# Token halves in the transition to the mLSTM, and column sums issued inside the second halves

## The chip, the core and the metric

The kernel runs on one core of a Trainium2 chip. Its engines are TensorE (PE in the profile; PEld is its weight load), VectorE (DVE), ScalarE (ACT), GpSimd (POOL) and SyncE (SP), whose queue starts the loads from HBM. Each engine runs its own instructions in the order in which they are written, and semaphores tie them together. The metric is the device time of one launch in microseconds, lower is better.

## The reference

`reference` runs one block of a first network and then one block of a second on 512 tokens of width 1024, all in float32. The first puts 16 meta tokens ahead of them, so it works on 528 tokens until its mixer is done.

```python
h = concat(meta_tokens, x)                                                     # 528 tokens
h = h + 0.5 * rmsnorm(swiglu(rmsnorm(h, gn[0]), ffn_w_in[0], ffn_w_out[0]), gn[1])  # feed-forward 0
u = rmsnorm(h, gn[2])
h = h + rmsnorm(mlstm_mixer(u, ...), gn[3])                                    # z = u @ w_in; conv; scan; y @ w_out
h = h + 0.5 * rmsnorm(swiglu(rmsnorm(h, gn[4]), ffn_w_in[1], ffn_w_out[1]), gn[5])  # feed-forward 1
x = h[16:]
h = x + 0.5 * swiglu_2(rms_norm(x, ffn1_norm), ...)                            # feed-forward 2
h = h + concat(mla, retention) @ w_o
h = h + 0.5 * swiglu_2(rms_norm(h, ffn2_norm), ...)                            # feed-forward 3
return rms_norm(h, final_norm)
```

## The kernel before

Activations lie transposed: width on the 128 partitions in `KD` = 8 tiles, tokens along the free axis, 528 of them (`TOK`) in feed-forward 0 and the mLSTM, 512 (`SEQ`) after. A tile k of a buffer is `buf[:, k*TOK : (k+1)*TOK]`. Each float32 product is made of three matmuls on rounded high and low parts (`whi`, `wlo` of the weights; `xhi`, `xlo` of the activations). Weights come in units of 128 x 1024 into four slots (`raw`); ACT makes `whi` (`split_to`, line 584), POOL makes `wlo` (`pool_lo`, line 457), and PE frees a slot when it is through with a unit (`unit_done`).

Between two stages lies a transition. The last products of a stage, tiles m = 0 to 7, are squared by ACT (`sq`, line 790), scaled and kept by DVE (line 1613), and the squares are added up in `acc` (line 1609). PE turns `acc` and the last `sq` into column sums, with `ones` as one moving column (matmuls of 128x1 in PSUM bank 7); ACT takes the root, DVE the reciprocal, and PE spreads it over the partitions by transposes of `rcol`. This gives r of the output norm. Then DVE multiplies a value tile by r (`wa`), the residual `hT` is updated (k = 0 on DVE, k = 1 to 7 on POOL), ACT makes `xhi` and the square of `hT` (`sqbuf`), DVE makes `xlo`, and PE multiplies the first units of the next stage by `xhi` and `xlo`. The squares in `sqbuf` give the next norm in the same way (sums, root, reciprocal, spread, `rbc`). It is applied behind the product, so the first products of the next stage need only `xhi` and `xlo`, while what DVE does with them needs `rbc`.

There are three transitions that the change touches. The **first** goes from feed-forward 0 to the mLSTM (`act_norm`, `dve_res`, `pool_res`, `sum_out`, `first_tiles`): whole tiles of 528 tokens, no product before r is in `rbc`; six adds of `sum_square` on DVE leave two squares to sum, 10 matmuls, behind projection 2. The **second** (mLSTM to feed-forward 1) and the **third** (feed-forward 1 to feed-forward 2) work by halves of 256 tokens. `out_steps` splits the last 3 output tiles (second) or the last one (third; table `SPLIT`), so that the first half of all tiles is complete while PE still makes the second; `act_transition`, `dve_transition`, `pool_transition` and `first_halves` hold the order, which is written out by hand. In `first_halves` PE first multiplies three units by the first halves of k = 0 to 7 (72 matmuls; the third unit lags by 3 k), with the sums and the spread of the second half's r in between, and then by the second halves (9 matmuls for each k, 72 in all). `sum_squares` gives the column sums of the next norm in two parts: 12 matmuls that wait for `norm_summed`, which DVE raises with the last of its three pair adds (`pair_squares`) behind all of `xlo`, and 8 matmuls on the last two squares. Before, part 0 stands behind k = 6 and part 1 behind k = 7; the spread stands in the fourth unit (`halved`).

What follows the first transition is the short convolution: DVE takes projection m from PSUM (line 1714, needs `rbc` and `unit_done`) and runs four more instructions on it, for m = 0 to 7; projection m >= 3 waits for `z_ready` of m - 3, and the value products wait for `z_ready` 6, 7 and 8. What follows the others is `dve_ffn`: `scaled` (line 1398), `conv_gate(0)` (line 1377, needs unit 0), `conv_up(0)` (line 1386, needs a SiLU of ACT, line 631), and on, until the loop of fast products (line 2508) starts.

## Time and profile before

| | |
|---|---|
| time, median of 3 runs | 2060.98 us (2059.63 to 2065.14) |
| the profiled execution's own time | 2064.66 us |
| its span | 2062.9 us |
| PE busy | 1983.3 us (96%) |
| DVE, ACT, POOL busy | 1190.0, 949.8, 915.8 us |
| granted PE clock, mean | 0.982 of full |

The span is what the profile covers; 1.8 us lie around it. The chain of waits is the chain that ended last, followed back from the end. A matmul that is recorded as float32 with 128x1 counts twice in the records (20 records for 10 matmuls). The first transition lies at 401 to 439 us, the second at 653 to 702 us, the third at 1028 to 1076 us. The clock column PEclk is 1.0 at 2.4 GHz and 0.5 at 1.2 GHz.

### The profile page before, as it was taken

What the parts mean: (1) busy time and instruction counts of PE and PEld (TensorE: products, weight loads), DVE (VectorE), ACT (ScalarE), POOL (GpSimd) and SP (SyncE); (2) the same over time, 40 slices, a digit from 0 to 9 for tenths busy, and PEclk for the clock granted to TensorE, in tenths of its full rate; (3) what the DMA queues carried; (4) which work ended last, traced back from release to release, by engine and by line L of the source; (5) the groups of instructions that cost most, each with busy time, mean ns of one, the idle gap of its engine ahead of it and who ended that gap; (6) DMA issues with size and microseconds to landing.
All of it is one profiled execution on the core that took longest, in us unless ns stands there. A gap on an engine that the chain in (4) does not pass through costs nothing.

```text
span 2062.9 us, 36078 instructions
## 1 busy us (share of the span) xinstructions
PE 1983.3 (96%) x13216; PEld 1774.7 (86%) x13216; DVE 1190.0 (58%) x1674; ACT 949.8 (46%) x1623; POOL 915.8 (44%) x528
## 2 busy tenths in 40 slices
PE   7899999899999989999999999999999999999998
PEld 7899999887778889987888999787776678999787
DVE  5766650186255777781068778314856637777611
ACT  4466642233423456662245666324426444666522
POOL 4244454444314445555453556454442033555542
PEclk9999999989999999999999999999999999999999
DMA  5133333213212133333322333334321022333331
GB/s 158 52 102 102 102 108 88 82 45 92 72 42 82 52 92 102 108 99 105 97 63 71 105 109 112 93 102 98 91 57 31 22 71 67 108 110 103 103 101 53
DMA packets 342479, 177.89 MB, mean 86 GB/s; under 512 B 18651, under 2 KB 338006, under 8 KB 342382
## 3 DMA queue, kind: packets, MB, share of 16 engines
q1 hardware_dynamic: 340528, 175.46, 29.5%
q8 instruction: 68, 1.11, 0.2%
q10 hardware_dynamic: 1854, 1.07, 0.2%
q14 instruction: 29, 0.24, 0.0%
HBM read 174.42 MB, written 2.10 MB: 86 GB/s over the span
## 4 chain that ended last, share of the span: by engine, by line
PE 82%; DVE 6%; issue 5%; ACT 3%; POOL 2%; DMA 0%; SPq 0%; ACTq 0%; POOLq 0%; DVEq 0%
PE ps L2268 40%; PE ps L2508 33%; POOL wlo L457 2%; PE ps L2333 1%; DVE E L1722 1%; DVE xop_f L1398 1%; PE ps L3000 1%; PE ps L2982 1%; PE ps L2959 1%; PE ps L2296 1%; DVE xop L1424 1%; PE ps L2363 1%; DMA raw<-in_ffn_w_in 0%; DVE wa L1697 0%; PE ps L2963 0%
## 5 line engine op out<-in xcount | busy, mean ns | idle before, releaser
L457 POOL TENSOR_TENSOR wlo<-raw,whi 128x1024 fp32r<-128x1024 f32 x192 | 484.8, 2535 | 662.3 <-ACT whi L584 661.8
L2508 PE MATMUL ps<-xop,whi 128*128 128x256 f32 (+1 forms) x4032 | 725.9, 283 | 16.4 <-issue 7.8
L2508 PEld LDWEIGHTS ps<-xop,whi 128*128 128x128 f32 x4032 | 623.8, 190 | 18.5 <-issue 9.5
L2508 PE MATMUL ps<-xop,wlo 128*128 128x256 f32 (+1 forms) x2016 | 569.1, 282 | 0.0
L2508 PEld LDWEIGHTS ps<-xop,wlo 128*128 128x128 f32 x2016 | 382.4, 190 | 0.0
L520 POOL TENSOR_TENSOR wlo<-raw,whi 128x512 fp32r<-128x512 f32 x212 | 283.8, 1343 | 215.1 <-ACT whi L661 215.1
L2268 PE MATMUL ps<-xop,whi 128*128 128x512 f32 (+2 forms) x1148 | 329.9, 348 | 13.4 <-POOL wlo L457 8.3
L584 ACT ACTIVATE whi<-raw 128x1024 fp32r<-128x1024 f32 x176 | 183.5, 1052 | 260.6 <-PE ps L2268 252.4
L2268 PE MATMUL ps<-xop,wlo 128*128 128x512 f32 (+2 forms) x902 | 284.7, 347 | 0.0
L2268 PE MATMUL ps<-xhi,whi 128*128 128x512 f32 (+2 forms) x672 | 225.4, 369 | 17.1 <-DVE xlo L1333 5.5
L2268 PEld LDWEIGHTS ps<-xop,whi 128*128 128x128 f32 x1148 | 197.1, 189 | 45.9 <-POOL wlo L457 5.3
L661 ACT ACTIVATE whi<-stage 128x512 fp32r<-128x512 f32 x216 | 136.6, 632 | 196.4 <-DVE stage L1448 118.2
L2268 PE MATMUL ps<-xlo,whi 128*128 128x512 f32 (+2 forms) x672 | 218.0, 358 | 0.0
L2268 PE MATMUL ps<-xhi,wlo 128*128 128x512 f32 (+2 forms) x672 | 217.6, 357 | 0.0
L2268 PE MATMUL ps<-hid_r,whi 128*128 128x512 f32 (+2 forms) x656 | 207.0, 347 | 0.0
L520 POOL TENSOR_TENSOR wlo<-stage,whi 128x512 fp32r<-128x512 f32 x72 | 93.4, 1297 | 198.6 <-ACT whi L661 198.6
L2268 PEld LDWEIGHTS ps<-xop,wlo 128*128 128x128 f32 x902 | 158.4, 189 | 22.6
L2268 PEld LDWEIGHTS ps<-xhi,whi 128*128 128x128 f32 (+1 forms) x672 | 121.1, 194 | 42.5 <-issue 18.9
L2268 PEld LDWEIGHTS ps<-xlo,whi 128*128 128x128 f32 (+1 forms) x672 | 121.1, 193 | 19.2 <-issue 2.2
L2268 PEld LDWEIGHTS ps<-xhi,wlo 128*128 128x128 f32 (+1 forms) x672 | 120.6, 193 | 18.1
L661 ACT ACTIVATE whi<-raw 128x512 fp32r<-128x512 f32 x216 | 133.6, 618 | 0.1
L2268 PEld LDWEIGHTS ps<-hid_r,whi 128*128 128x128 f32 x656 | 115.4, 189 | 16.6
(377 smaller groups left out, 2744.2 us busy)
## 6 DMA issues: line engine op xcount, KB each, us to landing
raw<-in_ffn_w_in SPq DMA_DIRECT2D x88, 512.0 KB, 3.7
raw<-in_ffn_w_gate SPq DMA_DIRECT2D x44, 512.0 KB, 3.7
raw<-in_ffn_w_up SPq DMA_DIRECT2D x44, 512.0 KB, 3.7
raw<-in_ffn_w_out SPq DMA_DIRECT2D x32, 512.0 KB, 3.9
raw<-in_ffn_w_down SPq DMA_DIRECT2D x32, 512.0 KB, 3.8
raw<-in_a_w_in SPq DMA_DIRECT2D x24, 512.0 KB, 3.7
raw<-in_w_in SPq DMA_DIRECT2D x19, 512.0 KB, 3.8
raw<-in_ffn_w_out SPq DMA_DIRECT2D x16, 384.0 KB, 3.3
```

Source lines behind the costliest of these rows:

```text
L457: pool.tensor_tensor(wlo[:, u % SLOTS, :], raw[:, u % SLOTS, :], whi[:, u % SLOTS, :].bitcast(F32), ALU.subtract).then_inc(lo_done, 1)
L520: pool.tensor_tensor(operand(wlo, i, name), source, operand(whi, i, name).bitcast(F32), ALU.subtract) \
L584: act.activation(whi[:, s, :], raw[:, s, :], ACT.Copy).then_inc(hi_done, 1)
L661: ins = act.activation(operand(whi, i, name), source, ACT.Copy)
L1398: ins = v.scalar_tensor_tensor(out=x_halves(k, n), scalar=gain(name, g0 + k), in0=hT[:, k * TOK + o:(k + 1) * TOK].rearrange("p (a n) -> p ...
L1424: v.tensor_tensor(x_operand(xop, name, 1, n), x_operand(xop_f, name, 1, n), x_operand(xop, name, 0, n).bitcast(F32), ALU.subtract).then_in ...
L1722: link(v, "dve", v.scalar_tensor_tensor(out=cacc(b), in0=zpad(b)[:, j:j + TOK], scalar=w[j], in1=cacc(b), op0=ALU.mult, op1=ALU.add))
L2268: ins = pe.matmul(o, lhs[l], x[r], start=first and n == 0, stop=last and n == 2)
L2296: ins = pe.matmul(ps[:, 7, c:c + 1], buf[:, o0 + o:o0 + o + P], ones[:, 0:1], start=q == 0, stop=q == len(sources) - 1, skip_group_check=True)
L2333: ins = pe.matmul(ps[:, b, HW * half:HW * (half + 1)], w[l], x[r], start=half == 0 and k == 0 and q == 0, stop=k == KD - 1 and q == 2, ski ...
L2363: ins = pe.matmul(ps[:, 7, c + 1:c + 2], sqbuf[:, k * TOK + META + c * P:k * TOK + META + (c + 1) * P], ones[:, 0:1], start=k == 0 and c = ...
L2508: ins = pe.matmul(ps[:, bank_, 0:h], w[l][:, k * P:(k + 1) * P], x[r][:, k * h:(k + 1) * h], start=start and k == 0 and q == 0, stop=k == ...
```

## The change

The first transition gets the halves of the other two: `SPLIT` has an entry for it, its first half holds 272 tokens (meta tokens and 256), its second 256. `first_tiles` and `sum_out` go from that place, and the first three mLSTM units run in `first_halves`; its matmuls there stay at 264 columns. The `sum_square` adds go, so the next norm's sums are 15 and 10 matmuls instead of 10. In all three transitions `sum_squares` part 0 moves behind k = 1, part 1 behind k = 2 and the spread behind k = 3 of the second halves. In the second, DVE makes the steps of the split output tiles ahead of the first `xlo`, with the `acc` adds early; ACT makes `xhi` of k = 0 between the two weight splits.

```diff
-SPLIT = {1: 3, 2: 1}
+SPLIT = {0: 1, 1: 3, 2: 1}
...
+    def half_span(n, half):
+        return ((0 if n == TOK else META, META + HW), (META + HW, TOK))[half]
+    def half_chunks(n, half):
+        first = [(0, 0)] if n == TOK and half == 0 else []
+        return first + [(c + 1, META + c * P) for c in (2 * half, 2 * half + 1)]
...
-        pool_lo(pool, u, U_M1 + AHEAD)
-        pool_res(pool, 0, TOK)
-        pool_transition(pool, 1, U_M1 + AHEAD, FFNS[1]["u0"])
+        pool_transition(pool, 0, u, U_M1)
+        pool_transition(pool, 1, U_M1 + SLOTS, FFNS[1]["u0"])
...
     def act_transition(...)
         for q in range(2):
             if q < SPLIT[i] - 1:
-                act_out_step(act, i, SEQ, False, u0, per, None, KD + q)
+                act_out_step(act, i, n, False, u0, per, None, KD + q)
             split_to(act, u_next + 1 + q - AHEAD)
-        x_hi(0, 0)
-        x_hi(1, 0)
+            x_hi(q, 0)
...
     def dve_transition(...)
-                if half == 0 and SPLIT[i] == 3 and k in (2, 4):
-                    step(KD + k // 2 - 1)
+                if half == 0 and k == 2:
+                    for p in range(KD, first):
+                        dve_out_acc(v, i, n, p)
+                        out_value(p)
+                    dve_out_acc(v, i, n, first)
                 if half == 0 and k == 5:
-                    step(first)
+                    out_value(first)
...
     def first_halves(...)
         for k in range(KD):
             for b, u in zip(banks, units):
                 ins = multiply(b, u, k, 1)
                 if k == KD - 1:
                     ins.then_inc(unit_done, 1)
-            if k >= KD - 2:
-                sum_squares(pe, norm, k - KD + 2)
+            if k in (1, 2):
+                sum_squares(pe, norm, k - 1, n)
+            if k == 3:
+                spread(pe, {R0: N1, R1: N2, R2: N3}[rms])
...
     def pe_mlstm(pe):
-        first_tiles(pe, 1, TOK, (0, 2), (u0, u0 + 1))
-        for m in range(2, 8):
+        first_halves(pe, 0, R0, 1, (0, 2, 4), (u0, u0 + 1, u0 + 2))
+        for m in range(3, 8):
             pe.wait_ge(lo_done, u0 + m + 1)
-            if m == 3:
-                spread(pe, N1)
-            if m >= 3:
-                pe.wait_ge(s["z_ready"], m - 2)
+            pe.wait_ge(s["z_ready"], m - 2)
             project(pe, 2 * (m % 3), TOK, u0 + m, None).then_inc(unit_done, 1)
-            if m == 2:
-                sum_norm(pe, 1, TOK)
...
     def pe_ffn(...)
-        whole = NU_DOWN - (len(FFN_PIECES) if i == 1 else 0)
+        whole = NU_DOWN - (len(FFN_PIECES) if i in (0, 1) else 0)
...
     def prog_tensor(pe):
         pe_ffn(pe, 0, 0, N0)
-        sum_out(pe, 0, TOK)
-        spread(pe, R0)
-        pe.wait_ge(r_s["ready"], r_at[R0]["ready"] + 2)
         pe_mlstm(pe)
```

How the change moves instructions is shown at three places. The first is PE at the end of the third transition's `first_halves`, before (`sqbuf` holds the squares of the residual, `rcol` the reciprocals):

```order
L2333 MATMUL ps<-xhi,wlo 128x256
L2363 MATMUL ps<-ones,sqbuf 128x1 [waits norm_summed]
L2363 MATMUL ps<-ones,sqbuf 128x1 x11
L2333 MATMUL ps<-xhi,whi 128x256 [waits norm_x_ready]
...
L2363 MATMUL ps<-ones,sqbuf 128x1 [waits norm_sq_ready]
L2363 MATMUL ps<-ones,sqbuf 128x1 x7
L2268 MATMUL ps<-xhi,whi 128x512 [waits ffn_banks_free,lo_done]
```

Here the 12 matmuls that wait for `norm_summed` have 63 of the 72 second-half matmuls ahead of them and 9 behind. The same instructions after the change:

```order
L2332 MATMUL ps<-xhi,wlo 128x256
L2364 MATMUL ps<-ones,sqbuf 128x1 [waits norm_summed]
L2364 MATMUL ps<-ones,sqbuf 128x1 x11
L2332 MATMUL ps<-xhi,whi 128x256 [waits norm_x_ready]
...
L2364 MATMUL ps<-ones,sqbuf 128x1 [waits norm_sq_ready]
L2364 MATMUL ps<-ones,sqbuf 128x1 x7
L2332 MATMUL ps<-xhi,whi 128x256 [waits norm_x_ready]
...
L2391 MATMUL ps<-ident,rcol 128x128 [waits rms_recip]
L2391 MATMUL ps<-ident,rcol 128x128 x3
L2332 MATMUL ps<-xhi,whi 128x256 [waits norm_x_ready]
```

Now 18 of the 72 stand ahead of the wait and 54 behind it; 9 lie between the two parts of the sums, 9 between them and the spread, and 36 behind the spread.

The second place is PE where feed-forward 0 ends. Before, the mLSTM's first product (`xhi`, 128x264) comes behind all sums and the whole spread, and also waits for `rbc` (`rms_ready`):

```order
L2268 MATMUL ps<-hid_r,whi 128x264 x2
L2268 MATMUL ps<-xop,wlo 128x264 x2
L2296 MATMUL ps<-ones,acc 128x1 [waits out_sq_ready,out_acc_done]
...
L2388 MATMUL ps<-ident,rcol 128x16 [waits rms_recip]
L2390 MATMUL ps<-ident,rcol 128x128 x4
L2268 MATMUL ps<-xhi,whi 128x264 [waits lo_done,norm_x_ready,rms_ready]
```

After the change the sums of the first half stand among the products (`xop`, `hid_r`) of the last tile's second half:

```order
L2260 MATMUL ps<-xop,wlo 128x256
L2305 MATMUL ps<-ones,acc 128x1 [waits out_sq_ready,out_acc_done]
L2305 MATMUL ps<-ones,acc 128x1 x2
L2305 MATMUL ps<-ones,sq 128x1 x3
L2260 MATMUL ps<-xop,whi 128x256
...
L2316 MATMUL ps<-ident,rcol 128x16 [waits rms_recip]
L2316 MATMUL ps<-ident,rcol 128x128 x2
L2260 MATMUL ps<-xop,whi 128x256
```

Six column sums and three transposes have gone into the last output tile; four and two more stand in `first_halves`.

The third place is DVE in the second transition, first halves (`y` is the kept output, `wa` the tile scaled by r). Before:

```order
L1613 TENSOR_SCALAR y<-ps,vec 128x256 [waits out_sq_ready]
L1652 SCALAR_TENSOR_TENSOR xlo<-hT,vec,xhi 128x256 [waits norm_hi_ready]
L1647 TENSOR_TENSOR wa<-y,ps 128x256 [waits res_h_ready]
L1652 SCALAR_TENSOR_TENSOR xlo<-hT,vec,xhi 128x256 [waits norm_hi_ready]
L1647 TENSOR_TENSOR wa<-y,ps 128x256 [waits res_h_ready]
L1609 TENSOR_TENSOR acc<-acc,sq 128x256 [waits out_acc_done,out_sq_ready]
L1613 TENSOR_SCALAR y<-ps,vec 128x256 [waits out_sq_ready]
L1652 SCALAR_TENSOR_TENSOR xlo<-hT,vec,xhi 128x256 [waits norm_hi_ready]
L1647 TENSOR_TENSOR wa<-y,ps 128x256 [waits res_h_ready]
L1609 TENSOR_TENSOR acc<-acc,sq 128x256 [waits out_acc_done,out_sq_ready]
```

After:

```order
L1623 TENSOR_SCALAR y<-ps,vec 128x256 [waits out_sq_ready]
L1614 TENSOR_TENSOR acc<-acc,sq 128x256 [waits out_acc_done,out_sq_ready]
L1623 TENSOR_SCALAR y<-ps,vec 128x256 [waits out_sq_ready]
L1614 TENSOR_TENSOR acc<-acc,sq 128x256 [waits out_acc_done,out_sq_ready]
L1664 SCALAR_TENSOR_TENSOR xlo<-hT,vec,xhi 128x256 [waits norm_hi_ready]
L1659 TENSOR_TENSOR wa<-y,ps 128x256 [waits res_h_ready]
```

Both `acc` adds stand ahead of the first `xlo`, where the second stood behind the third.

## Rows read from the trace of the kernel before

**Rows 1.** The page: busy time of each engine, and the chain's shares.
```profile
PE 1983.3 (96%) x13216; PEld 1774.7 (86%) x13216; DVE 1190.0 (58%) x1674; ACT 949.8 (46%) x1623; POOL 915.8 (44%) x528
...
PE 82%; DVE 6%; issue 5%; ACT 3%; POOL 2%; DMA 0%; SPq 0%; ACTq 0%; POOLq 0%; DVEq 0%
```

**Rows 2.** Chain of waits, 400 to 445 us: start, length, what.
```profile
...
402.21 2.38 PE ps L2296 x20
...
434.04 2.14 PE ps L2296 x20
```

**Rows 3.** Timeline of PE: start, length, form, count, idle before, releaser.
```profile
400.96 0.40 PE L2268 MATMUL ps<-xop,wlo 128*128 128x264 f32 x2
...
411.21 0.78 PE L2268 MATMUL ps<-xhi,whi 128*128 128x264 f32 x2 [5.25 <-issue]
...
479.15 0.50 PE L2268 MATMUL ps<-whi,xhi 128*128 128x512 f32 x1 [0.30 <-DVE E L1714]
```

**Rows 4.** Timeline of DVE, first projection read by the mLSTM.
```profile
438.87 0.71 DVE L1714 TENSOR_TENSOR E<-ps,rbc 128x528 f32<-128x528 f32 x1 [1.62 <-issue]
```

**Rows 5.** Chain of waits, 1045 to 1072 us, transition after feed-forward 1.
```profile
1047.64 10.92 PE ps L2333 x90
1058.56 2.67 PE ps L2363 x24
1061.23 1.72 PE ps L2333 x9
1062.94 3.21 PE ps L2363 x16
1066.15 2.77 PE ps L2268 x6
1068.92 0.87 PE ps L2390 x4
```

**Rows 6.** Timeline of PE, the same transition and its end.
```profile
1037.75 0.30 PE L2333 MATMUL ps<-xhi,whi 128*128 128x256 f32 x1
...
1107.86 0.48 PE L2508 MATMUL ps<-xop,whi 128*128 128x256 f32 x2 [2.96 <-issue]
```

**Rows 7.** Timeline of DVE, the same transition.
```profile
1056.44 1.89 DVE L1341 TENSOR_TENSOR sqbuf<-sqbuf 128x512 f32<-128x512 f32 x3
...
1076.31 0.68 DVE L1386 TENSOR_TENSOR wb<-wa,ps 128x512 f32<-128x512 f32 x1
```

**Rows 8.** Timeline of ACT, the same transition.
```profile
1070.30 2.94 ACT L584 ACTIVATE whi<-raw 128x1024 fp32r<-128x1024 f32 x3
1073.26 1.28 ACT L631 ACT_TABLE_LOAD   x1
1074.56 0.63 ACT L631 ACTIVATE wa<-wa 128x512 f32<-128x512 f32 x1
```

**Rows 9.** Windows: busy us of each engine, granted clock (PEclk), DMA share, GB/s.
```profile
64.00:68.00 4.00, 4.00 (x20) 4.00 (x19) 4.00 (x5) 0.00 (x0) 0.00 (x0) 0.50 0.00 0
68.00:72.00 4.00, 4.00 (x34) 4.00 (x33) 3.25 (x5) 0.65 (x1) 0.00 (x0) 0.96 0.00 0
...
1060.00:1064.00 4.00, 4.00 (x27) 4.00 (x27) 0.00 (x0) 0.00 (x0) 0.00 (x0) 0.70 0.02 4
1064.00:1068.00 4.00, 4.00 (x16) 3.61 (x16) 0.19 (x2) 0.27 (x1) 0.00 (x0) 0.50 0.00 0
...
1072.00:1078.00 6.00, 6.00 (x27) 4.88 (x26) 5.96 (x9) 5.97 (x8) 6.00 (x3) 1.00 0.38 111
```

**Rows 10.** Timeline of PE, a long wait in feed-forward 0.
```profile
62.64 0.78 PE L2268 MATMUL ps<-xhi,whi 128*128 128x264 f32 x2 [4.70 <-DVE wb L1386]
```

**Rows 11.** Timeline of PE, transition after the mLSTM.
```profile
666.97 1.01 PE L2313 MATMUL ps<-ones,acc 128*128 128x1 f32 x4 [3.22 <-DVE acc L1609]
```

**Rows 12.** Timeline of DVE, transition after the mLSTM.
```profile
682.86 1.89 DVE L1341 TENSOR_TENSOR sqbuf<-sqbuf 128x512 f32<-128x512 f32 x3
...
702.07 0.68 DVE L1386 TENSOR_TENSOR wb<-wa,ps 128x512 f32<-128x512 f32 x1
```

More of the change, by code:

```diff
@@ L832, in act_transition @@
             x_hi(k, 1)
[L833 removed]
+            act.activation(tile(sqbuf, k, n), tile(hT, k, n), ACT.Square).then_inc(s["sq_ready"], 1)
     def act_mlstm(act):
@@ L2254, in out_bank @@
     def out_bank(i, p, n, half=None):
+        if half is not None and n == TOK:
+            return ps[:, 4, 0:META + HW] if half == 0 else ps[:, 1, 0:HW]
         if half is not None:
```

170 lines of the change are left out of this document (78 added, 92 removed).

## The prediction

> **What bounds the kernel now.** The page comes first: PE is busy for 96% of the span and makes 82% of the chain that ended last; DVE makes 6% of it [rows 1]. So only places where PE waits, or runs at the lower clock, can give or lose time. I then read, for each transition, the chain of waits, the timelines of PE, DVE and ACT, and the granted clock.
>
> First transition. PE ends feed-forward 0 at 401.4 and starts the mLSTM's first product at 411.21 behind 5.25 us of idle time [rows 3]; it sums for 2.38 us ahead of that and for 2.14 us (to 436.2) behind projection 2 [rows 2]. What ends the transition is not PE but `rbc`: DVE takes projection 0 at 438.87 [rows 4]. From there DVE works through eight projections, and at 479.15 PE still waits for one of them [rows 3]. The mLSTM therefore moves with that start of DVE, which I call the mark; it is the quantity that the first transition changes.
>
> Third transition (the second has the same order). PE starts at 1037.75 [rows 6]. Ninety matmuls run without a gap from 1047.64 to 1058.40, 0.12 us each, then come the sums [rows 5]. Of the 90, 63 are second halves, so 27 belong to the first; the second halves start at 1047.64 + 27 x 0.12 = 1050.9 and k = 0 and 1 are done at 1053.0. DVE adds the squares last, from 1056.44 to 1058.33 [rows 7]. The transition's own end is on DVE: `conv_up(0)` at 1076.31 [rows 7], and PE still waits 2.96 us at 1107.86 for what follows it on DVE [rows 6]. That start of `conv_up(0)` is the mark here; in the second transition it lies at 702.07 [rows 12].
>
> **The change part by part.**
>
> The common part, `sum_squares` behind k = 1: the 12 matmuls wait for `norm_summed`. The change moves nothing of what raises it, since the pair adds stay behind all `xlo` on DVE and the squares behind `xhi` on ACT. PE gets there at 1053.0 and the semaphore comes at 1058.4: a new wait of 5.4 us on PE, and behind it in PE's order stand 54 of the 72 second-half matmuls, the sums, the spread and the next unit. Before, these 5.4 us were filled with products. What it buys is an earlier `rbc`.
>
> What the clock does then decides. Behind a wait of 5.25 us two matmuls of 264 columns took 0.78 us, where two took 0.40 ahead of it [rows 3]. Behind one of 4.70 us, at 62.64 [rows 10], the clock was 0.50, 1.2 GHz, in the window from 64 to 68 and back at 0.96 in the next one, so some 5.5 us after PE resumed [rows 9]. In the third transition, with no long wait, the clock fell behind the 2.67 us of sums (0.70, then 0.50) and was back only in the window from 1072, some 5.9 us after the last sum at 1066.15 [rows 5, 9]: one-column matmuls with 9 products among them did not hold or restore 2.4 GHz. So I take 1.2 GHz from the end of the new wait until about 5 us after the last sum. The sums then cost 3.21 / 16 = 0.20 us a record against 2.67 / 24 = 0.11 at full clock, a product 0.215: between the 0.19 of nine of which some were still fast [rows 5] and twice 0.12.
>
> The Trainium skill says the same of the direction, and against this change (page "TensorE: Matmul & The Clock Gate", Part 1, section "What's actually happening"): the default state is throttled and activity releases the throttle, so a hole in a busy stretch costs more than its length. It does not say whether one-column matmuls count as activity. If they do, the case is rival B below; the sum would then be -2 us instead of +11. Rows 5 and 9 speak against it, but nothing here shows sums right behind a wait this long.
>
> Third transition, worked out: sums 1058.4 + 24 x 0.20 = 1063.2; k = 2 (9 x 0.215) 1065.1; 16 x 0.20: 1068.3; k = 3: 1070.2; spread 0.87 [rows 5]: 1071.1. Of the 36 left, unit 0's last product is the 30th: 10 at 0.215 until the clock is back at about 1073.3, 20 at 0.12: 1075.7. Only then may ACT split the next three units: 2.94 us, table load 1.28 us, SiLU 0.63 us, 4.9 us in all from 1070.30 to 1075.19 [rows 8], so SiLU ends at 1080.6 and `conv_up(0)` starts at 1080.7 instead of 1076.31: **+4.4 us**. `rbc` itself comes at 1071.8 and no longer matters: before, the splits waited for the root on ACT, now they wait for unit 0 on PE. The PE side, all later units pushed by some 7 us, still fits: it has 2.96 us of wait at 1107.86 [rows 6], and DVE is 4.4 us later too. Bounds: 0 if DVE's chain has room that I do not see; +7 if PE's own delay counts in full.
>
> Second transition. Before, PE waits 3.22 us for `acc` [rows 11]. Both adds now stand ahead of the first `xlo`, so this wait goes; what is late next is `xlo` of k = 2 beside POOL's weight split, as in the third transition. I move everything there forward by 3 us (bounds 0 and 3.22): the squares, added at 684.75 [rows 12], are added at 681.8. From there it is the third transition again: mark 681.8 + (1080.7 - 1058.4) = 704.1 against 702.07: **+2.0 us**.
>
> First transition. PE's products stay as many (the last output tile as 66 matmuls of 272 and 66 of 256 columns instead of 132 of 264), but 12 records of sums (1.3 us) and three transposes (0.6 us) move into it, so it ends at 403.3 instead of 401.4. The halves then run as in the third transition: first halves done 1050.9 - 1037.75 = 13.1 us later, 0.2 for 264 columns, 416.6; squares added 1058.4 - 1037.75 = 20.6 us later, 0.5 for 272 and 528 columns, 424.4. The wait is again 5.5 us. Sums are 15 and 10 matmuls, 30 and 20 records, instead of 20 records: 424.4 + 6.0, + 9 x 0.22, + 4.0, + 9 x 0.22, + 1.1 for the spread = 439.5; 9 more at 0.22 and 21 at 0.12: unit 0 is done at 444.0, and the mark moves from 438.87 to 444.0: **+5.1 us**. The 5.25 us of idle time before the first product does go; it comes back as this wait, as 30 records more of sums and as a longer time at 1.2 GHz. With the old placement of the sums (first sums behind k = 6, where PE arrives at 424.3 and waits for nothing) they would end at 424.4 + 3.3 + 1.1 + 4.0 = 432.8, and the mark would follow 2.7 us later, as 438.87 follows 436.2 [rows 2, 4]: 435.5, 3.4 us ahead of now. So it is the placement that loses, not the halves. Bounds: -2.3 at full clock throughout, +8 if the clock stays low to the end of the halves.
>
> The rest costs nothing on the path: ACT's `xhi` of k = 0 comes earlier than PE can use it, POOL gets the same adds in two halves while PE is at the last tile, DVE loses six adds of squares that ended ahead of the sums. SP's loads wait for slots as before.
>
> Sum: 5.1 + 2.0 + 4.4 = 11.5 us on the profiled execution's own 2064.66, that is 2076.2. That execution is 3.7 us above the median of 2060.98, so the predicted time is 2060.98 + 11.5 = 2072.5 us.
>
> **The rivals.**
>
> A, full clock: the wait is there, but PE comes out of it at 2.4 GHz. Third transition: sums 2.67, products 1.08, sums 1.8, products 1.08, spread 0.5, 30 products 3.6 from 1058.5: 1069.2; plus 4.9: mark 1074.1, -2.2. Second: 681.9 + 10.7 + 4.9 = 697.5, -4.6. First: 424.5 + 3.3 + 1.1 + 2.2 + 1.1 + 0.6 + 3.7 = 436.5, -2.4. Together -9.2: 2051.8 us. For it speaks only that the clock fell some way into the sums and not at once [rows 5, 9]; against it both waits near 5 us. 0.10.
>
> B, sums count as work: low for some 5.5 us behind the wait, then full. Third: 4.8 of sums and 0.7 low, then 0.7 + 1.8 + 1.1 + 0.5 + 3.6 = 1071.6, mark 1076.5, 0. Second 699.4, -2.5. First 439, 0. Together about -2.4: 2058.6 us. 0.13.
>
> C, no cost behind feed-forward starts: the second and third transitions lose nothing because work behind `conv_up(0)` has room, and only the first counts: +5.1, 2066.1 us. Against it, PE waits 2.96 us at the end of that work [rows 6], so DVE sets its length and a later start of DVE moves it. 0.15.
>
> **How the numbers follow.** 0.62 for the forecast, whose own range is 2067 to 2079: the clock back between 4 and 6 us behind the sums (2 us for each transition), and the run's own spread of 2 to 3 us. A, B and C have 0.10, 0.13 and 0.15. For 8 in 10 I take 2056 to 2079. A measurement here tells 0.3%, 6.2 us, from no change: faster is below 2054.8 (A: 0.10), slower is above 2067.2 (the forecast less its low edge, and the upper part of C: 0.65), and the rest, 0.25, is within.
>
> **What would show it.** In the profile of the changed kernel: a PE wait of 5 to 6 us on DVE's square adds ahead of `sqbuf` sums, three times; a granted clock of 0.5 around and behind those sums; 24 records of sums in the third transition in 4.8 us, not 2.7; no wait for `acc` in the second; DVE's first projection about 5 us later counted from the end of feed-forward 0's last full tile; ACT's three weight splits behind unit 0 and not behind the root. It would be wrong if PE came to the sums later than I think (a wait under 3 us), if the clock were full right behind the wait, or if `conv_up(0)` moved and the first fast products did not.

## The result and the profile after

The changed kernel takes 2086.7 us (median of 4 runs, 2085.3 to 2087.4) against 2062.8 for the kernel before (median of 4 runs): ratio 1.0106, interval 1.009 to 1.0122. Run again with the experiments (below) it is 1.0098, 1.0081 to 1.0116. The forecast was 2072.5 us with a range of 2056 to 2079: slower, as said, but by 20 to 24 us and not by 11.5, and outside the range.

The page of the changed kernel, the lines that answer to [rows 1]:

```profile
span 2083.2 us, 36164 instructions
...
PE 1998.3 (96%) x13246; PEld 1787.8 (86%) x13246; DVE 1193.8 (57%) x1689; ACT 951.6 (46%) x1631; POOL 918.8 (44%) x535
...
PE 80%; DVE 6%; issue 5%; ACT 4%; POOL 3%; DMA 0%; SPq 0%; ACTq 0%; POOLq 0%; DVEq 0%
```

The span is 20.3 us longer than before (2062.9), but PE is busy for only 15.0 us more, with 30 instructions more. So most of what was lost is PE working slower, not PE waiting. The table of PE's waits names the one new wait (columns: who waits for whom, us in total, times, longest):

```profile
PE ps L2364 <- DVE sqbuf L1347: 15.4, 3, 5.2
```

Three waits of 5.1 us for the square adds, one in each transition. The `acc` wait [rows 11] is gone, and so is the 5.25 us ahead of the mLSTM's first product [rows 3].

The chain of waits of the third transition, which answers to [rows 5] and [rows 8] (columns: start, length, what):

```profile
1070.98 5.28 PE ps L2364 x24
1076.26 2.13 PE ps L2332 x9
1078.39 3.21 PE ps L2364 x16
1081.59 2.13 PE ps L2332 x9
1083.72 0.85 PE ps L2391 x4
1084.58 5.03 PE ps L2332 x36
...
1089.94 1.99 ACT whi L589 x2
...
1091.95 1.28 ACT L636
...
1093.25 0.64 ACT wa L636
...
1093.91 0.70 DVE wb L1392
```

24 records of sums take 5.28 us, where they took 2.67 [rows 5]; nine products 2.13 us, 0.237 each. ACT's weight splits, which before began right behind its `rbc`, now wait for PE to end unit 0's second halves (timeline of ACT):

```profile
1088.98 2.96 ACT L589 ACTIVATE whi<-raw 128x1024 fp32r<-128x1024 f32 x3 [3.77 <-PE ps L2332]
```

The clock of the same stretch, in windows (columns: window, its length, busy us of PE, weight loads, DVE, ACT, POOL, granted clock, DMA share, GB/s):

```profile
1066.00:1070.00 4.00, 0.00 (x0) 0.00 (x0) 3.02 (x7) 3.12 (x7) 1.86 (x3) 0.89 0.00 0
1070.00:1086.00 16.00, 15.02 (x70) 15.03 (x71) 1.88 (x7) 0.86 (x2) 0.00 (x0) 0.50 0.00 1
1086.00:1090.00 4.00, 4.00 (x33) 3.92 (x32) 3.05 (x5) 1.02 (x2) 0.00 (x0) 0.98 0.00 0
```

So the clock stays at 1.2 GHz for 16 us, although PE is busy in all of them but the first (the end of its wait).

**Where the 20.3 us are.** The mark is DVE's first projection in the first transition and `conv_up(0)` in the others. I call the time from PE's first half product (L2333 before, L2332 after) to the mark the length of a transition. Second: 702.07 - 662.09 = 39.98 before, 712.08 - 668.85 = 43.23 after. Third: 1076.31 - 1037.75 = 38.56 before, 1093.91 - 1050.31 = 43.60 after. The first has no such start before; there I align DVE's instructions of feed-forward 0's output (330 to 384 us), where the changed kernel is 0.42 us early, and its mark (444.32) is 5.45 us late: +5.87, that is a length of 41.61 after against 35.7 before. Then, in order of time:

| place | us |
|---|---|
| up to the last tile of feed-forward 0 | -0.4 |
| first mark | +5.9 |
| lower clock behind the wait for the last projection, at 484 | +1.5 |
| mLSTM to second start | -0.2 |
| second mark | +3.25 |
| from `conv_up(0)` to the first fast product behind its 2.96 us wait | +1.0 |
| lower clock behind a wait of 1.77 us at 955 | +1.6 |
| third mark | +5.0 |
| from `conv_up(0)` to the first fast product | +1.0 |
| the rest (lower clock at 1712 to 1724 the largest) | +1.7 |

The first row hides two things that nearly cancel. DVE's first `ybuf` row (at 302.53 before) is 1.09 us late in the changed kernel, for a reason that no run shows. Behind it the clock of the profile before falls at 304 and that of the changed kernel does not, which gives 1.5 us back (rows below, in the part on the prediction).

The three places behind the marks, in rows. First PE's wait in the value products of the mLSTM for DVE's last projection (the expectation of e7 calls it the wait for the first gate), which was 0.30 us [rows 3], and the windows around it, in the changed kernel:

```profile
484.55 0.50 PE L2260 MATMUL ps<-whi,xhi 128*128 128x512 f32 x1 [2.05 <-DVE E L1707]
```

```profile
480.00:484.00 4.00, 2.50 (x13) 1.46 (x10) 3.93 (x4) 0.09 (x1) 2.50 (x1) 1.00 0.18 24
484.00:488.00 4.00, 3.45 (x10) 2.56 (x11) 3.86 (x6) 1.02 (x2) 0.00 (x0) 0.68 0.31 114
488.00:492.00 4.00, 4.00 (x17) 2.65 (x16) 3.86 (x5) 2.40 (x3) 2.41 (x1) 0.90 0.00 0
```

Then feed-forward 1's down projection. The same wait of 1.77 us stands in both kernels; only behind that of the changed kernel does the clock fall. After (timeline of PE, windows):

```profile
954.98 0.50 PE L2260 MATMUL ps<-xop,whi 128*128 128x512 f32 x1 [1.77 <-DVE ybuf L1623]
```

```profile
952.00:956.00 4.00, 2.23 (x10) 1.49 (x9) 1.83 (x2) 2.98 (x4) 2.27 (x1) 1.00 0.02 4
956.00:960.00 4.00, 4.00 (x12) 3.13 (x11) 3.43 (x3) 0.00 (x0) 2.88 (x2) 0.57 0.47 132
```

Before, the window behind the same wait (at 943.98):

```profile
944.00:948.00 4.00, 4.00 (x17) 3.27 (x18) 4.00 (x3) 0.57 (x1) 3.90 (x2) 1.00 0.39 109
```

And DVE behind `conv_up(0)` of the second transition, before and then after (timeline of DVE):

```profile
704.82 3.42 DVE L1410 TENSOR_TENSOR xop_f<-xop_f 128x1024 f32<-128x1024 f32 x1
708.16 1.21 DVE L1411 TENSOR_TENSOR xop_f<-xop_f 128x1024 f32<-128x1024 f32 x1
```

```profile
713.55 3.43 DVE L1416 TENSOR_TENSOR xop_f<-xop_f 128x1024 f32<-128x1024 f32 x1
716.91 3.43 DVE L1417 TENSOR_TENSOR xop_f<-xop_f 128x1024 f32<-128x1024 f32 x1
```

The second add takes 3.43 us and not 1.21. After the change both run while GpSimd (POOL) splits weights; before, only the first did (timeline of POOL, before and then after):

```profile
701.94 5.22 POOL L457 TENSOR_TENSOR wlo<-raw,whi 128x1024 fp32r<-128x1024 f32 x2
```

```profile
710.67 8.58 POOL L469 TENSOR_TENSOR wlo<-raw,whi 128x1024 fp32r<-128x1024 f32 x3
```

Of these 2.2 us, 1.3 come back in the instruction ahead of the adds (`hid_f`, 0.83 us instead of 2.12), so the fast products are 1.0 us later behind the mark. In every profile with early sums in the second and third transitions, e14 apart, the two adds take 3.43 us each, and in those with the sums behind k = 6 or 7 about 3.42 and 1.21.

### The profile page after: what moved, and what is told of

It reads as the page before. It is cut to its first block, busy times and chain, and to the rows that moved or that the text cites. A ratio compares the mean times of both kernels' runs of the same rounds, so it can differ in the third digit from the quotient of the medians.

```text
span 2083.2 us, 36164 instructions
## 1 busy us (share of the span) xinstructions
PE 1998.3 (96%) x13246; PEld 1787.8 (86%) x13246; DVE 1193.8 (57%) x1689; ACT 951.6 (46%) x1631; POOL 918.8 (44%) x535
## 4 chain that ended last, share of the span: by engine, by line
PE 80%; DVE 6%; issue 5%; ACT 4%; POOL 3%; DMA 0%; SPq 0%; ACTq 0%; POOLq 0%; DVEq 0%
PE ps L2260 38%; PE ps L2508 33%; POOL wlo L469 3%; PE ps L2364 1%; PE ps L2332 1%; DVE E L1715 1%; PE ps L2995 1%; PE ps L2977 1%; DVE xop L1430 1%; PE ps L2954 1%; POOL hT L486 1%; ACT whi L589 1%; DVE xlo L1664 1%; DVE xop_f L1404 1%; DMA raw<-in_ffn_w_in 0%
## 5 line engine op out<-in xcount | busy, mean ns | idle before, releaser
L2260 PE MATMUL ps<-xop,whi 128*128 128x512 f32 (+3 forms) x1148 | 333.2, 348 | 13.6 <-POOL wlo L469 8.4
L2260 PE MATMUL ps<-xop,wlo 128*128 128x512 f32 (+3 forms) x902 | 288.1, 347 | 0.0
L2260 PE MATMUL ps<-xhi,whi 128*128 128x512 f32 (+2 forms) x624 | 212.4, 370 | 8.6 <-DVE wb L1392 4.7
L2260 PE MATMUL ps<-hid_r,whi 128*128 128x512 f32 (+3 forms) x656 | 209.7, 347 | 0.0
L2260 PE MATMUL ps<-xlo,whi 128*128 128x512 f32 (+2 forms) x624 | 206.4, 360 | 0.0
L2260 PE MATMUL ps<-xhi,wlo 128*128 128x512 f32 (+2 forms) x624 | 206.1, 360 | 0.0
L2260 PEld LDWEIGHTS ps<-xhi,whi 128*128 128x128 f32 (+1 forms) x624 | 111.7, 191 | 32.8 <-issue 13.5
L2260 PEld LDWEIGHTS ps<-xlo,whi 128*128 128x128 f32 (+1 forms) x624 | 111.9, 191 | 19.4 <-issue 2.2
L1628 DVE SCALAR_TENSOR_TENSOR hT<-ps,hT 128x512 f32<-128x512 f32 x24 | 16.6, 690 | 194.5 <-PE ps L2260 194.5
```

Of the source, the lines that this page charges most:

```text
L2260: ins = pe.matmul(o, lhs[l], x[r], start=first and n == 0, stop=last and n == 2)
```

## The experiments

Each ratio compares 5 to 12 runs of the kernel with 11 to 27 of the kernel before on the same chip. Lengths of transitions are from each one's profile, as defined above; "-" is where no halved first transition exists.

| kernel | ratio (95%) | first | second | third |
|---|---|---|---|---|
| before | 1 | 35.7 | 39.98 | 38.56 |
| changed | 1.0106 (1.009, 1.0122) | 41.61 | 43.23 | 43.60 |
| changed again (e8) | 1.0098 (1.0081, 1.0116) | 41.13 | 42.90 | 43.47 |
| e1 late sums | 0.9979 (0.9967, 0.9992) | 32.04 | 38.05 | 38.60 |
| e2 early sums alone | 1.0069 (1.0053, 1.0085) | - | 45.09 | 43.11 |
| e3 `acc` adds alone | 1.0003 (0.9991, 1.0015) | - | 38.48 | 38.55 |
| e4 waits filled | 1.0058 (1.0041, 1.0075) | 40.03 | 39.73 | 39.78 |
| e5 sums behind 5 and 6 | 1.0008 (0.9994, 1.0021) | 36.32 | 38.43 | 37.35 |
| e6 late, spread earlier | 0.9972 (0.9957, 0.9987) | 34.96 | 36.45 | 35.79 |
| e7 early in the first only | 1.0025 (1.0014, 1.0037) | 41.57 | 38.02 | 37.12 |
| e9 short wait filled | 1.0104 (1.0089, 1.0119) | 41.56 | 43.15 | 43.71 |
| e10 before, spread earlier | 0.9993 (0.9982, 1.0003) | - | 38.72 | 36.13 |
| e11 sums interleaved | 0.998 (0.997, 0.9991) | 31.78 | 36.62 | 36.90 |
| e12 one add more, first | 0.9964 (0.9951, 0.9978) | 29.76 | 37.80 | 35.81 |
| e13 all sums in one row | 0.9963 (0.995, 0.9975) | 29.76 | 34.65 | 37.18 |
| e14 POOL's splits cut | 1.0065 (1.0052, 1.0078) | 42.62 | 42.89 | 43.20 |
| e15 one row, adds in all | 0.9956 (0.9944, 0.9969) | 29.66 | 35.01 | 34.80 |

A length is from one execution, and the same instructions do not always take the same time. With late sums the first transition took 34.96 us in e6 and 32.04 in e1, the third 38.60 in e1 and 37.12 in e7, the second 36.45 in e6 and 37.80 in e12, each pair with the same instructions in that transition. With early sums the repeats (changed, e8, e9) agree within 0.5 us, though e14's first transition, which its edit does not touch, took 1.0 us more than the longest of them. So a difference of 1.5 us between two kernels with late sums, or of 3 in their first transition, is not shown by a pair of profiles.

**e1, the sums back behind k = 6 and 7.** The central question: the halves or the placement.

```diff
-            if k in (1, 2):
-                sum_squares(pe, norm, k - 1, n)
-            if k == 3:
-                spread(pe, {R0: N1, R1: N2, R2: N3}[rms])
+            if k >= KD - 2:
+                sum_squares(pe, norm, k - KD + 2, n)
```

(with the spread where it was before: ahead of k = 2 of the next unit, in the mLSTM ahead of the `z_ready` wait of m = 3).

> The changed kernel with its halves in the first transition and its new places of the acc adds and of x_hi, but the column sums back behind k = 6 and 7 of the second halves and the spread in the next unit. Theory (the placement of the sums loses, the halves gain): no wait for the square adds; DVE takes projection 0 of the mLSTM about 3.4 us earlier than before, conv_up(0) of the second transition about 3 us earlier (the acc wait of 3.22 us is gone), the third where it was: -6, about 2057 us, 30 us below the changed kernel. Rival (the halves themselves, or the earlier acc adds beside POOL's hT halves, lose): no gain on before, 2063 to 2075 us. Rival (short waits in other places that lower the clock): marks as in the theory, but the time 2 to 5 us above 2057.

Measured 0.9979, about -4.3 us, where -6 was expected (inside the interval, -1.7 to -6.8). The first mark is 3.7 us earlier than before (3.4 expected), the second 1.9 (3 expected), the third where it was. All of the other parts of the change together are a gain; the early sums turn it into a loss of 20.

**e2, only the early sums, in the kernel before.** The same edit the other way round, in the second and third transitions.

```diff
-            if k >= KD - 2:
-                sum_squares(pe, norm, k - KD + 2)
+            if k in (1, 2):
+                sum_squares(pe, norm, k - 1)
+            if k == 3:
+                spread(pe, {R1: N2, R2: N3}[rms])
```

> The kernel before with one part of the change: the sums behind k = 1 and 2 and the spread behind k = 3 in the second and third transitions; the first transition and the acc adds as before. Theory (placement): a wait of about 5.3 us on the square adds in each, sums at 0.20 us a record, conv_up(0) later by 5.0 us in the third as in the changed kernel and by 5 in the second, since there the acc wait of 3.2 us stays, and 1 us more in each behind conv_up(0): +12, about 2075 us. Rival (the first transition's halves are what loses in the changed kernel): +3 or less, 2063 to 2066 us.

1.0069, +14 us where +12 was expected; marks +5.1 and +4.6. The rival (nearly all of the loss in the first transition) falls.

**e3, only the `acc` adds and `x_hi` moved.**

```diff
-                if half == 0 and SPLIT[i] == 3 and k in (2, 4):
-                    step(KD + k // 2 - 1)
+                if half == 0 and k == 2:
+                    for p in range(KD, first):
+                        dve_out_acc(v, i, SEQ, p)
+                        out_value(p)
+                    dve_out_acc(v, i, SEQ, first)
                 if half == 0 and k == 5:
-                    step(first)
+                    out_value(first)
```

> The kernel before with another part of the change alone: the acc adds ahead of the first xlo on DVE and x_hi(0), x_hi(1) inside ACT's loop. Theory: PE's wait of 3.22 us for acc in the second transition goes, in its place come waits for xlo of some 2.2 us as in the third, and the square adds come earlier: conv_up(0) 1 to 3 us earlier there, nothing in the third: -2, about 2061 us. Rival (POOL's weight split beside DVE takes the gain back): 0, 2063 us.

The second transition is 1.5 us shorter (39.98 to 38.48), the third unchanged; in the time (1.0003) 1.5 us can't be seen. PE's wait of 3.22 us for `acc` is gone, but PE now waits for `xlo` four times instead, 2.62 us in all (timeline of PE):

```profile
664.52 0.36 PE L2340 MATMUL ps<-xhi,whi 128*128 128x256 f32 x1 [0.42 <-DVE xlo L1656]
...
668.56 0.39 PE L2340 MATMUL ps<-xhi,whi 128*128 128x256 f32 x1 [0.78 <-DVE xlo L1656]
...
671.79 0.38 PE L2340 MATMUL ps<-xhi,whi 128*128 128x256 f32 x1 [0.23 <-DVE xlo L1656]
...
674.30 0.39 PE L2340 MATMUL ps<-xhi,whi 128*128 128x256 f32 x1 [1.19 <-DVE xlo L1656]
```

So most of the removed wait comes back as waits. What does go is the low clock behind the 3.22 us: 6 us at 0.50 before, none in e3 (windows, before and then e3):

```profile
666.00:672.00 6.00, 5.03 (x23) 5.04 (x24) 4.19 (x11) 2.87 (x6) 3.76 (x5) 0.50 0.29 87
```

```profile
666.00:672.00 6.00, 4.89 (x37) 4.24 (x36) 4.80 (x9) 3.28 (x7) 6.00 (x6) 1.00 0.30 87
```

By the chains of waits the sums of the next norm start 20.70 us behind PE's start instead of 23.33, and 1.1 us of these 2.6 are lost again, since the clock falls earlier in them (nine products 1.73 us instead of 1.16, the last 16 records 3.21 instead of 2.75). The mark moved by half of the 3 us that I took for this wait.

**e4, the three waits filled with products.** Is it the wait, or what the clock does behind it?

```diff
+            if k == 1:
+                for b, u in 4 * list(zip(banks, units)) + [(banks[0], units[0]), (banks[1], units[1])]:
+                    multiply(b, u, 1, 1)
             if k in (1, 2):
                 sum_squares(pe, norm, k - 1, n)
```

> The changed kernel with 42 more matmuls of 256 (272) columns behind k = 1 of the second halves, where PE waits for the square adds in each of the three transitions; they repeat the product of k = 1 and add it to the same sums again, so the output is not the reference's. They take 42 x 0.12 = 5.0 us and fill the wait of 5.15 us. Theory (the wait lowers the clock): the first 24 records of sums cost 0.11 us each and not 0.20, the clock falls behind them, and each mark comes about 3.1 us earlier than in the changed kernel: -9, about 2077 us. Rival (the sums are slow in this place for another reason, such as DVE and ACT in the same banks): 0.20 us a record and 2086 us. Rival (without the wait the clock holds through all sums): some 6 us a transition, 2068 us.

1.0058 against 1.0106 and 1.0098: 8 to 10 us less, with 126 matmuls more and the sums starting no earlier. The chain of the third transition:

```profile
1066.49 2.84 PE ps L2367 x24
1069.33 1.43 PE ps L2332 x9
1070.76 3.21 PE ps L2367 x16
1073.97 2.13 PE ps L2332 x9
1076.10 0.85 PE ps L2394 x4
1076.95 4.31 PE ps L2332 x36
```

The first 24 records take 2.84 us (5.28 behind the wait); the clock then falls all the same and the last 16 take 3.21 in both. The marks are 3.5 and 3.8 us earlier than in the changed kernel in the second and third, 1.6 in the first, whose 50 records outlast the full clock. This shows the clock behind the wait as a cause. It also parts it from the wait itself: in e4 PE is held as long, by products of no use, and the third transition still takes 1.2 us more than before (39.78 against 38.56), so of the 5.0 us lost there the clock makes 3.8.

**e8, the changed kernel again, and e9, one short wait filled.**

```diff
+            if i == 1 and j == 6:
+                for _ in range(7):
+                    x = hid_hi_tile(HID_ORDER[0], n)
+                    pe.matmul(ps[:, 6, 0:n], x[:, 0:P], x, start=True, stop=True, skip_group_check=True)
             pe.wait_ge(out_s["v_ready"], v_at + m + 1)
```

> The changed kernel as it is, once more. The marks as in its first trace to 0.1 us, counted from PE's start of each transition. Open is the clock behind short waits: in the first trace it fell to about 0.6 behind a wait of 2.05 us at 484 and one of 1.77 us at 955, where other kernels with a wait of 1.77 us kept 1.00. If that belongs to the execution, the drop at 955 is absent here; if it belongs to the program, both drops come back. Ratio 1.009 to 1.012.

> The changed kernel with 7 more matmuls of 512 columns (7 x 0.233 = 1.63 us, into bank 6, whose value nobody reads) ahead of PE's wait of 1.77 us for ybuf in feed-forward 1's down projection, at 955. Both profiles of the changed kernel show a clock of 0.57 to 0.68 from 956 to 960 and the next stretch 1.6 us longer than before. Theory (the short wait lowers the clock there): no low clock behind 955, 1.6 us less, ratio 1.009. Rival (the drop comes from something else, such as the 0.95 us wait at 941 or the power of that stretch): it stays, ratio 1.010.

In e8 the lengths agree with the first profile to 0.5 us (not the 0.1 I expected), and both drops are back: 0.80 and 0.77 from 484 to 492, 0.68 from 956 to 960. In e9, with 7 products in the place of the wait, the second one is gone:

```profile
952.00:956.00 4.00, 3.85 (x17) 2.82 (x16) 1.23 (x2) 2.81 (x4) 1.67 (x1) 1.00 0.02 4
956.00:960.00 4.00, 4.00 (x19) 3.23 (x18) 4.00 (x3) 0.17 (x1) 3.53 (x2) 1.00 0.47 131
```

The time did not fall (1.0104): 1.6 us is below what the interval resolves, and in e9's profile the fast loop ahead of it is 1.2 us longer, for which I have no reason. Nor does this one profile show that the wait is needed for the drop. Of the 16 profiles with the 1.77 us wait unfilled, 6 show the drop (changed, e6, e8, e10, e14, e15) and 10 don't, among them e4 and e7, both with early sums. e10 is the kernel before with one small edit, so the drop does not belong to the change. Behind the wait of 2.05 us for the last projection the clock falls in 5 of 6 profiles (changed, e4, e7, e8, e9; not e14). Whether the clock falls behind such a wait is not settled by its length.

**e7, the early sums in the first transition only.** The edit of e1 under `if n == SEQ`.

> The changed kernel with the sums behind k = 6 and 7 in the second and third transitions, as in e1, and behind k = 1 and 2 with the spread behind k = 3 in the first alone. Theory: the first mark (projection 0 on DVE) as in the changed kernel, 9.6 us later than in e1 counted from PE's start of the transition, and a low clock for about 1.5 us behind PE's wait for the first gate at 484; the rest as e1: +9.6 to +11, ratio 1.003. Rival (part of the first mark's delay is taken up by the mLSTM): +5 or less, ratio 1.000.

1.0025 against e1's 0.9979, 9.5 us more; first length 41.57, also 9.5 us more. So the mLSTM takes up nothing of it that the intervals would show.

**e5, the sums behind k = 5 and 6, the spread behind 7.**

```diff
-            if k in (1, 2):
-                sum_squares(pe, norm, k - 1, n)
-            if k == 3:
+            if k in (5, 6):
+                sum_squares(pe, norm, (5, 6).index(k), n)
+            if k == 7:
                 spread(pe, {R0: N1, R1: N2, R2: N3}[rms])
```

> The changed kernel with the sums behind k = 5 and 6 of the second halves and the spread behind k = 7, in all three transitions. From the traces of the changed kernel and of the one with the sums behind 6 and 7: the square adds come 20.7 us behind PE's start of the transition, PE is at the end of k = 5 at 19.6, so the wait is about 1.1 us. Theory (a short wait costs little, the long wait and the low clock behind it make the loss): the sums start at the same time as with 6 and 7, the spread comes about 0.7 us earlier, marks 0 to 1 us earlier than there; 2056 to 2063 us, ratio to before 0.995 to 0.999. Rival (any wait ahead of the sums lowers the clock for them at once): 0.20 us a record from the first one, each mark some 3 us later: ratio 1.002.

1.0008, so above e1 by 6 us; neither forecast holds as a whole. The waits are 0.73, 0.90 and 0.89 us. In the second and third transitions the clock is full right behind them (24 records in 2.88 and 2.84 us), against the rival. The third is 1.25 us shorter than in e1, as the theory has it; the first is 4.3 longer: there the clock is 0.50 from 428 on, in the middle of the first 30 records. e6 below shows the same early fall there with no wait at all, so the wait is not shown as its cause.

**e6, late sums and the spread one k earlier; e10, that edit alone in the kernel before.**

```diff
         def halved(k):
-            if k == 2:
+            if k == 1:
                 spread(pe, rms)
```

> The kernel with the sums behind k = 6 and 7, and the spread of the second and third transitions one k earlier, behind the first 3 matmuls of the next unit and not behind 6 (0.45 us each at 1.2 GHz). Theory (conv_up(0) there follows rbc, since ACT's splits wait for the root and not for unit 0): rbc 1.36 us earlier, marks of the second and third 1.3 us earlier each, ratio about 0.9966, 2.7 us below the run with the spread behind 6. Rival (the matmuls behind the spread only take its place and ACT's splits wait for unit 0 or its weights): 0, ratio 0.998.

> The kernel before with one edit: the spread of the second and third transitions behind 3 matmuls of the next unit and not behind 6. Nothing of the change is in it. Theory (the edit is worth the same with and without the change): conv_up(0) 1.4 to 2.8 us earlier in the second and third, ratio 0.9985, so that of the gain of e6 (0.9972) about half is the change's halves and acc adds. Rival (e6's gain is all from the spread): ratio 0.997.

e6 has 0.9972: the second and third are 1.6 and 2.8 us shorter than in e1. e10 has 0.9993 with 1.3 and 2.4 us. e6's gain over e10, 0.0021 or 4.3 us, is what the halves and the `acc` adds are worth, the same as in e1; the gain of the earlier spread itself is inside the intervals in both. But e6's first transition is 2.9 us longer than e1's, with the same instructions in the same order. Windows of e1, then of e6:

```profile
424.00:428.00 4.00, 4.00 (x38) 4.00 (x36) 1.58 (x3) 0.00 (x0) 0.00 (x0) 1.00 0.00 0
428.00:432.00 4.00, 4.00 (x34) 4.00 (x33) 0.00 (x0) 0.00 (x0) 0.00 (x0) 0.90 0.00 0
```

```profile
424.00:428.00 4.00, 4.00 (x37) 4.00 (x35) 1.88 (x4) 0.04 (x1) 0.00 (x0) 1.00 0.00 0
428.00:432.00 4.00, 4.00 (x20) 4.00 (x21) 0.00 (x0) 0.00 (x0) 0.00 (x0) 0.53 0.00 0
```

By the shares of the window from 428 to 432 the clock falls at about 431.2 in e1 and 428.2 in e6, counted from starts 0.3 us apart. Why it falls 3 us earlier in one stays open; it is worth 3 us.

**e11, the first part of the sums among the products of k = 7.** One or two one-column matmuls ahead of each product instead of a row of 12 (15) behind k = 6.

> The kernel of e6 with the first part of the sums (12 one-column matmuls, 15 in the first transition) not in a row behind k = 6 but one or two at a time between the 9 products of k = 7. Theory (a column sum is idle time for the clock wherever it stands, since the share of products stays the same): the clock falls as in e6, marks within 0.5 us of it, ratio 0.997. Rival (only long rows of sums lower the clock): records at 0.11 us to the end of the first part, the clock full until the second, marks 1 to 2 us earlier each, ratio 0.995.

0.998 (e6: 0.9972), the second and third 0.2 and 1.1 us longer: no gain. The first is 3.2 us shorter, which is e1's length again, and so may be the same earlier or later fall of the clock. In all three the sums among products ran at full clock (30 records and 9 products in 4.46 us in the first, as in e1), as the rival has it, and the clock fell within about 1 us of the start of the row that follows. The marks that the rival hoped for did not come.

**e12, e13 and e15: fewer sums, and in one row.** e12, in the first transition, against e6:

```diff
-            if k >= KD - 2:
-                sum_squares(pe, norm, k - KD + 2, n)
+            if k == (KD - 1 if n == TOK else KD - 2):
+                sum_squares(pe, norm, 0, n)
+            if k == KD - 1:
+                sum_squares(pe, norm, 1, n)
...
-        for k in ((0, 2, 4), (6, 7))[part]:
+        for k in ((0, 4) if n == TOK else (0, 2, 4), (6, 7))[part]:
```

with one more `tensor_tensor` on DVE (`sqbuf` 0 += `sqbuf` 2) behind the pair adds. e13 puts both parts behind k = 7 in all three; e15 has the further add in all three.

> The kernel of e6 with one more add of squares on DVE in the first transition alone (the sums of tiles 0-1 and 2-3 together), and its column sums all behind k = 7: 20 one-column matmuls (40 records) and not 25 (50 records). Theory (the length of the sums at a low clock is what the first mark pays): 10 records less at 0.11 to 0.21 us, first mark 1 to 2 us earlier than in e6 (34.96 us behind PE's start of the transition), the rest as e6, ratio 0.9965. Rival (all sums now run at the low clock behind k = 7, or the later add makes PE wait): no gain, 0.997 to 0.998.

> The kernel of e12 with the sums of the second and third transitions also in one row behind k = 7 (40 records) and not in two (24 behind k = 6, 16 behind k = 7). Theory (the clock falls some 5 us into the stretch of sums and stays low behind it, so what is summed in a row first is summed at 0.11 us a record and the products at the low clock are fewer): 1.1 us of products and 4.4 us of sums, 5.5 us from the end of k = 6, against 6.2 to 6.9 in e6; conv_up(0) 0.5 to 1.4 us earlier in each, ratio 0.9955. Rival (the row of 40 records falls to the low clock in its middle): 0, ratio 0.9965 or above.

> The kernel of e13 with the further add of squares on DVE in the second and third transitions too: 16 one-column matmuls (32 records) in one row and not 20 (40). Theory: 8 records of 0.11 us less in each, 0.9 us earlier marks than e13, ratio about 0.995. Rival (the add, 0.7 us later, makes PE wait or ends too late): as e13 or above.

The chain of e12's first transition:

```profile
415.20 12.37 PE ps L2337 x99
427.58 4.37 PE ps L2369 x40
431.95 0.02 issue
431.97 0.28 ACT rcol L602
```

40 records in 4.37 us, 0.109 each: the clock falls only behind them. The first mark is 5.2 us earlier than in e6, more than the 1 to 2 expected, since the last 20 records too are now summed at 2.4 GHz; 2.9 of the 5.2 are e6's early fall, and against e1 it is 2.3. The first transition took 29.66 to 29.76 us in all three kernels with this row. In e13 the row of 40 took 4.36 us in the second transition and 6.37 in the third, where the clock fell in its middle (the rival), so e13 (0.9963) is no better than e12 (0.9964) by the time. In e15 the rows of 32 took 4.24 and 4.01 us, with the clock falling in them, and the first row of 40 took 4.37. e15 is the lowest of these: 2054.6 us against 2062.7, ratio 0.9956, about 9 us below the kernel before and 30 below the changed one; its interval and those of e12 and e13 overlap.

**e14, GpSimd's weight splits cut.**

```diff
-            pool.tensor_tensor(wlo[:, u % SLOTS, :], raw[:, u % SLOTS, :], whi[:, u % SLOTS, :].bitcast(F32),
+            pool.tensor_tensor(wlo[:, u % SLOTS, 0:w], raw[:, u % SLOTS, 0:w], whi[:, u % SLOTS, 0:w].bitcast(F32),
...
-        pool_lo(pool, u0 + (SLOTS if i in (1, 2) else AHEAD), u0 + 2 * NCONV)
+        pool_lo(pool, u0 + (SLOTS if i in (1, 2) else AHEAD), u0 + 2 * NCONV, 64 if i in (1, 2) else 1024)
```

> The changed kernel with GpSimd's weight split (wlo) of the 4 units behind unit 3 of feed-forwards 1 and 2 cut to 64 of its 1024 columns, so those low weights are wrong and the output is not the reference's. Theory (behind conv_up(0) DVE's second xop_f add takes 3.43 us and not 1.21, since GpSimd's weight splits come later there and run beside it): both adds take 1.2 us, the first fast product comes 31.5 us or less behind conv_up(0) in both transitions (before: 31.5 and 31.6; changed kernel: 32.5), and 2 to 6 us less in all, ratio 1.007 to 1.009. Rival (the later start of the fast loop comes from ACT's or PE's order): still 32.5 us, ratio 1.010.

```profile
1092.63 1.22 DVE L1416 TENSOR_TENSOR xop_f<-xop_f 128x1024 f32<-128x1024 f32 x1
1093.77 1.22 DVE L1417 TENSOR_TENSOR xop_f<-xop_f 128x1024 f32<-128x1024 f32 x1
```

Both adds take 1.22 us without GpSimd beside them. PE's 2.96 us wait ahead of the fast products shrinks to 0.77, and they come 30.1 and 30.0 us behind `conv_up(0)`, where the changed kernel has 32.5 and the kernel before 31.5. The ratio is 1.0065, 7 to 8 us below the changed kernel. So GpSimd beside DVE, and not ACT's or PE's order, makes these adds slow. The cut takes away more than the change had added: 2.4 us in each, of which 1.0 is the change's by the traces; its profile also lacks the drop behind the wait at 484 (1.5 us). What the same cut is worth in the kernel before was not tried.

## Why the prediction was wrong

**The new wait of 5.4 us on PE: right.** It measured 5.12, 5.15 and 5.14 us.

**The clock behind it: right.** 0.50 from 424 to 440, and from 1070 to 1086. Sums cost 0.20 to 0.22 us a record (forecast 0.20), the nines of products 0.237 to 0.243 each (forecast 0.215). e4 shows it as a cause. The sentence from the Trainium skill ("TensorE: Matmul & The Clock Gate", Part 1, "What's actually happening"), that activity is what releases the throttle, agrees in direction: filled with products, the same 5 us made the next 24 records 2.4 us shorter. Rivals A and B fall: the clock did not come back while the sums ran.

**"It is the placement that loses, not the halves": right.** e1, e2 and e7 show it from both sides; late sums in the first transition put its mark 3.7 us earlier in e1, 3.4 forecast. How much depends on when the clock falls: in e6 it is 0.7.

**First mark, +5.1: right** in place (444.0 forecast, 444.32), +5.9 if the 0.4 us by which the run was ahead is counted. **Third mark, +4.4: nearly right,** +5.0; the first 24 records at 0.22 and not 0.20 (0.5 us) and 18 products at 0.237 and not 0.215 (0.4 us) make the difference, less 0.2 in unit 0's last products.

**Second mark, +2.0: mis-sized,** +3.25. The failed step is "I move everything there forward by 3 us (bounds 0 and 3.22)". In the changed kernel the square adds end 20.6 us behind PE's start and not 22.7 [rows 12], so they moved forward by 2.0 us; the marks of e3 and e1 moved by 1.5 and 1.9. The waits for `xlo`, which the sentence before it names, were not priced. The trace before has them in its third transition, with 0.82, 0.25 and 1.19 us.

**"The rest costs nothing on the path": the step that failed.** Two costs of the change stood behind the marks, and a third that comes with the execution.

- The fast products came 1.0 us later still in the second and third transitions, since GpSimd's splits moved against DVE's adds (e14). The sum stopped at `conv_up(0)` and so took what follows it on DVE to keep its length; it does not.
- PE's wait for DVE's last projection, at 479.15 before [rows 3], grew from 0.30 to 2.05 us, since DVE's projections were delayed by 5.4 us and PE's products by 3.7, and the clock fell behind it in 5 of 6 profiles: 1.5 us.
- A wait of 1.77 us that the change does not touch had no drop behind it in the profile before and one in both profiles of the changed kernel: 1.6 us. e10 has the drop without the change, so it is not the change's. The profile before showed what such a wait can do, in its twin in feed-forward 0 (timeline of PE, window):

```profile
303.35 0.51 PE L2268 MATMUL ps<-xop,whi 128*128 128x264 f32 x2 [1.77 <-DVE ybuf L1613]
```

```profile
304.00:308.00 4.00, 4.00 (x22) 4.00 (x22) 3.80 (x3) 0.00 (x0) 3.23 (x2) 0.59 0.47 135
```

In the changed kernel's first profile this window has 1.00, and in its second (e8) the clock falls there too. Of all 17 profiles 13 have this drop. Such drops come and go with the execution, so a sum of marks can't hold them; they belonged in the width of the range.

Together, in the two profiles: marks +14.2 (forecast 11.5), the fast products +2.0, the drop at 484 +1.5. The drops at 955 (+1.6) and 304 (-1.5) cancel, and the rest, some 2.6 us, has no cause that a run shows.

**The base, 2060.98.** I took 3.7 us off, since the profiled execution stood above the median of three runs. The later medians of the kernel before, over 11 to 27 runs, are 2062.7 to 2065.5 us: the profiled execution was a usual one and the three runs were low. This is 2 to 4 us of the 14 by which the number missed. The steps named above are 6.2 (2.7 in the marks, 2.0 and 1.5 behind them); no run assigns the remaining 4 to 6.

**Rival C** (only the first transition counts) falls: e2, with early sums in the other two alone, costs 14 us, and between e7 and the changed kernel lie 15 to 17.

## What to carry to other kernels

In these transitions the clock fell in the column sums or right behind them and did not come back while they ran. So put them behind as much product work as there is, make them few (one more add on DVE took 10 of 50 records away in e12), and keep them from standing behind a wait of several microseconds. Whether they stand in one row or in two made no difference that the time shows. When a step is moved so that PE arrives ahead of its operand, price the whole stretch from the wait to some 5 us behind the last sum at half speed, and then ask once more what moves against what behind the point where the sum ends. And compare lengths from two profiles only after a repeat has shown how far the same instructions differ. A base of three runs is worth no correction of a few microseconds.

## What the runs showed of the hardware

- Behind a long wait, a stretch of one-column fp32 matmuls with products between did not bring 2.4 GHz back: PE was busy for 15.02 of the 16 us from 1070 to 1086 at a granted clock of 0.50. Spreading part of them among products (e11) made no difference to the time. At 2.4 GHz a record costs 0.109 us (e12), at 1.2 GHz 0.20.
- Behind a wait of 3.22 us the clock was 0.50 from 666 to 672; with waits of at most 1.19 us in its place (e3) it stayed at 1.00.
- Behind waits of 1.77 to 2.06 us the clock fell for some 3 us in 24 of 39 cases (6 of 16 at the place of 955, 5 of 6 at that of 484, 13 of 17 at that of 304) and stayed full in the others, for the same instructions; it costs 1.5 us when it falls.
- In the same row of sums the clock fell about 3 us earlier in one execution (e6) than in another (e1), and the mark came 2.9 us later.
- A DVE add of 128x1024 takes 1.22 us alone (e14) and 3.43 beside GpSimd's splits (changed kernel).
